# Seven block products instead of eight in six gate slabs of the mix part

## The reference

```python
u = rms_norm(h, mix_norm)
proj = u @ w_in                      # q, k, v, pool input, and 2 x 1024 gate columns
gates = sigmoid(proj[..., o:].reshape(B, S, 2, D_MODEL))
y_attn = dilated_mixture_attention(q, k, v) @ w_branch_attn      # 256 -> 1024
y_pool = multiscale_pool(pz, pool_w, pool_scale) @ w_branch_pool # 512 -> 1024
merged = gates[:, :, 0] * y_attn + gates[:, :, 1] * y_pool
h = h + merged @ w_out
```

## Time and profile before

| what | value |
|---|---|
| median of three executions | 1877.08 us |
| profiled execution, its own time | 1877.25 us |
| its span (first to last instruction) | 1875.0 us |
| TensorE busy | 1860.3 us, 99% |
| VectorE busy | 1294.7 us, 69% |
| ScalarE busy | 867.4 us, 46% |
| GpSimd busy | 46.5 us, 2% |
| granted TensorE clock, mean | 0.998 |

### The profile page before, as it was taken

One profiled execution on the slowest core, in us unless ns is written; L12 is line 12 of the kernel. 1 busy time (PEld: TensorE's weight loads), 2 busy tenths in 40 slices (PEclk: granted clock), 3 DMA queues, 4 the chain that ended last, 5 costly groups with the idle time before them and its releaser, 6 DMA issues.

```text
span 1875.0 us, 26603 instructions
## 1 busy us (share of the span) xinstructions
PE 1860.3 (99%) x10599; PEld 1626.1 (87%) x10599; DVE 1294.7 (69%) x1728; ACT 867.4 (46%) x1132; POOL 46.5 (2%) x60
## 2 busy tenths in 40 slices
PE   9999999999999999999999999999999999999997
PEld 7998998888888888988998888888888888888886
DVE  8875887887566578866888746364646786666666
ACT  6643664436353236633653242333336654454445
POOL 0000000000000000000000000000000000000000
PEclk9999999999999999999999999999999999999999
DMA  6734763311112235744753223221221222212213
GB/s 212 184 126 123 194 169 110 117 59 62 61 62 93 98 112 141 190 145 115 190 153 123 98 83 107 72 89 67 93 89 66 90 71 87 90 67 89 89 67 90
DMA packets 44382, 203.61 MB, mean 109 GB/s; under 512 B 5136, under 2 KB 6192, under 8 KB 32128
## 3 DMA queue, kind: packets, MB, share of 16 engines
q1 hardware_dynamic: 37088, 177.23, 27.6%
q0 software_dynamic: 6768, 24.50, 6.8%
q10 hardware_dynamic: 432, 0.56, 0.1%
HBM read 198.60 MB, written 3.67 MB: 108 GB/s over the span
## 4 chain that ended last, share of the span: by engine, by line
PE 96%; DVE 2%; ACT 1%; issue 0%; DMA 0%; DVEq 0%; ACTq 0%
PE acc L2205 22%; PE acc L2207 22%; PE acc L2206 22%; PE acc L2212 6%; PE acc L2211 6%; PE acc L2213 6%; PE att L2205 2%; PE att L2206 2%; PE att L2207 2%; PE att L2211 1%; PE att L2213 1%; PE att L2212 1%; PE acc L2442 1%; PE acc L2467 1%; DVE w_lo L1232 0%
## 5 line engine op out<-in xcount | busy, mean ns | idle before, releaser
L1232 DVE TENSOR_TENSOR w_lo<-raw,w_hi 128x2048 fp32r<-128x2048 f32 x126 | 286.9, 2277 | 76.6 <-ACT w_hi L580 75.8
L2205 PE MATMUL acc<-x_hi,w_hi 128*128 128x512 f32 x808 | 318.3, 394 | 0.9 <-DVE x_lo L1295 0.6
L2207 PE MATMUL acc<-x_hi,w_lo 128*128 128x512 f32 x808 | 314.9, 390 | 0.0
L2206 PE MATMUL acc<-x_lo,w_hi 128*128 128x512 f32 x808 | 314.7, 389 | 0.0
L580 ACT ACTIVATE w_hi<-raw 128x2048 fp32r<-128x2048 f32 x126 | 239.2, 1899 | 128.6 <-PE acc L2207 113.9
L2205 PEld LDWEIGHTS acc<-x_hi,w_hi 128*128 128x128 f32 x808 | 151.7, 188 | 36.0 <-issue 2.1
L2206 PEld LDWEIGHTS acc<-x_lo,w_hi 128*128 128x128 f32 x808 | 151.8, 188 | 32.4 <-issue 1.4
L2207 PEld LDWEIGHTS acc<-x_hi,w_lo 128*128 128x128 f32 x808 | 151.7, 188 | 31.9
L2205 PE MATMUL acc<-g_hi,w_hi 128*128 128x512 f32 x352 | 137.0, 389 | 0.0
L2206 PE MATMUL acc<-g_lo,w_hi 128*128 128x512 f32 x352 | 137.0, 389 | 0.0
L2207 PE MATMUL acc<-g_hi,w_lo 128*128 128x512 f32 x352 | 136.9, 389 | 0.0
(11 more groups left out here) (440 smaller groups left out, 4485.1 us busy)
## 6 DMA issues: line engine op xcount, KB each, us to landing
raw<-in_ret_head SPq DMA_DIRECT2D x24, 1024.0 KB, 4.8
raw<-in_ffn_down SPq DMA_DIRECT2D x32, 704.0 KB, 4.0
raw_c<-in_ffn_seven SPq DMA_DIRECT2D x37, 512.0 KB, 5.3
raw<-in_ffn_seven SPq DMA_DIRECT2D x33, 512.0 KB, 4.6
raw<-in_ffn_seven POOLq DMA_DIRECT2D x33, 512.0 KB, 7.5
raw<-in_ffn_seven SPq DMA_DIRECT2D x37, 256.0 KB, 4.5
raw<-in_mix_gate SPq DMA_DIRECT2D x8, 1024.0 KB, 4.8
raw<-in_ret_out SPq DMA_DIRECT2D x8, 1024.0 KB, 4.8
```

What stands on the lines that cost most here:

```text
L1232: tt(w_lo[:, slot, at:at + cols], raw[:, slot, 0:cols], w_hi[:, slot, at:at + cols].bitcast(F32), ALU.subtract).then_inc(w_ready, 1)
L2205: mm(dst, still[0], move[0], start=first, stop=False)
L2206: mm(dst, still[0], move[1], start=False, stop=False)
L2207: return mm(dst, still[1], move[0], start=False, stop=last)
```

## The change

Six of the eight gate slabs (those of the second, third and fourth pair) take seven products. Their weights are laid out in quarters (`mix_seven`), and fetched in three transfers a slab instead of one, with one accumulating transfer by GpSimd. The first pair stays as it was on TensorE.

- x's combinations for the mix: ScalarE writes gain x h, sorted, to `mix_top` and `mix_low` (8 activations); GpSimd makes four two-input operations of 1024 columns (`mix_forms`); ScalarE and VectorE split the results.
- The two sums of weights of each of the six slabs are made by GpSimd (`add_sums` in its program), not by VectorE as in the feed-forward parts.
- Of a branch slab only the 1536 columns that are used are split, not 2048. Three of its four results stay in PSUM (`att`) until they are multiplied.
- Each gate's early and late 256 tokens come from the four combinations of products (`blocks_of`), are scaled by the norm, and pass the sigmoid in two activations.
- SP holds back a branch slab, and the first slab of the output projection, until GpSimd's sums of the slot's last slab are made (`sum4_ready`).
- `dynamic_dma_scratch_size=4096` makes the room for descriptors of GpSimd's transfers smaller, and two unused tensors grow by 12 KB a partition.

```diff
@@ sync
+            for j in range(1, DC // 2):
+                if j > 1:
+                    sp.wait_ge(sum4_ready, v.k - 1)
+                fetch(dram["mix_branch"][j], 12 * BLK)
+                for k in range(2):
+                    w = dram["mix_seven"][2 * j + k - MIX_PLAIN]
+                    fetch_pair(w)
+                    fetch_one(w)
+                    if j == 1:
+                        sp.wait_ge(seg_done, FFN_SEGS[0] + GATES_FROM + 1)
+                    fetch_c(w)
+            sp.wait_ge(sum4_ready, v.k)
@@ gpsimd
+            def mix_forms():
...
+                pool.wait_ge(mix_x_ready, DC)
+                add(mix_form[:], b11, b12, ALU.subtract).then_inc(mix_formed, 1)
+                pool.wait_ge(mix_formed, 1)
+                add(b12, b12, b22, ALU.subtract).then_inc(mix_formed, 1)
+                add(b11, mix_form[:], b22, ALU.add).then_inc(mix_formed, 1)
+                pool.wait_ge(mix_formed, 3)
+                add(b21, b21, b11, ALU.subtract).then_inc(mix_formed, 1)
...
+            mix_forms()
+            for j in range(1, DC // 2):
+                for k in range(2):
+                    slab = FC + 2 * DC + BRANCH_FROM + 3 * j + 1 + k
+                    add_pair(dram["mix_seven"][2 * j + k - MIX_PLAIN], slab)
+                    add_sums(slab)
+                    v.next()
@@ scalar
+            for c in range(DC):
+                mix_x(c)
+            s.next(3)
+            sigmoid(0)
+            s.next(2)
+            u.next(2)
+            prep()
+            split_form(1, xt_hi[:, 0, :, :], mix_form[:])
...
+                for k in range(2):
+                    two, one = acc[:, u.k % BANKS, :], acc[:, (u.k + 1) % BANKS, :]
+                    split_sum4()
+                    if k:
+                        sigmoid_late()
+                        sigmoid_early()
+                    snap(1, t(0)[:, EARLY], two[:, EARLY])
+                    if k:
+                        split_val(m_hi[:, 2 * j, :], t(4))
+                    snap(2, t(0)[:, LATE], one[:, EARLY])
+                    if k == 0:
+                        split_pair()
+                    elif j < DC // 2 - 1:
+                        prep(12 * BLK)
+                    else:
+                        prep()
+                    snap(3, t(1)[:, EARLY], two[:, EARLY])
@@ vector
+                for k in range(2):
+                    if k:
+                        last_rows(0)
+                        late_product(pool_first)
+                    low_c()
+                    if k:
+                        early_product(attn)
+                    low_sum4()
+                    if k:
+                        low_mixed(2 * j)
...
+                    link(blocks_of(side))
+                    tt(t(3), t(3), rstd[:], ALU.mult).then_inc(val_ready, 1)
@@ tensor
+            for j in range(1, DC // 2):
+                w = slab()
+                branch_part(side_bank(), w, 2, (pool_hi, pool_lo), 4).then_inc(att_full, 1)
+                branch_part(side_bank(), w, 0, (o_hi, o_lo), 2).then_inc(att_full, 1)
+                branch_part(side_bank(), w, 8, (pool_hi, pool_lo), 4).then_inc(att_full, 2)
+                b.next()
+                side = att[:, (b.k - 1) % BANKS, EARLY]
+                project(w, 6, (o_hi, o_lo), 2)
+                for k in range(2):
+                    seven(6 if j == 1 and k == 0 else None, side)
```

More of the change, by code:

```diff
@@ L36 @@
 SNAPS = 4
+MIX_PLAIN = 2
+MIX_SEVEN = DC - MIX_PLAIN
 QUART = SLAB // PARTS
@@ L531, in _, with add_pair @@
                 pool.dma_start(dst if name == "signs" else dst[:], dram[name]).then_inc(const_landed, 16)
+            def add_pair(w, slab, ahead=None):
+                third = v.k % RING
+                pool.wait_ge(pair_landed[third], v.landed())
+                pool.dma_start(pair_place(slab % RING, ahead), w[:, QUART:3 * QUART],
+                               accum_op=ALU.add).then_inc(added_pair[third], 16)
             def add_pairs(name, full, first_slab):
@@ L932, in sigmoid, with mix_x @@
                 nc.scalar.activation(t(4 + o), t(4 + o), ACT.Sigmoid).then_inc(fn_ready, 1)
-            for i in range(DC // 4):
-                for j in range(2):
-                    if i or j:
-                        prep()
[L938 to L953, removed]
+            def mix_x(c):
+                dst = (mix_top if c < TB else mix_low)[:, c % TB, :]
+                nc.scalar.activation(sorted_row(dst), row_to_sort(h[:, c, :]), ACT.Copy,
+                                     scale=gains[:, 1, c:c + 1]).then_inc(mix_x_ready, 1)
@@ L1431, in seven, with blocks_of @@
                     low_one()
+                if ahead is not None:
+                    dve.wait_ge(pair_free, v.k)
+                blocks_of(att[:, snaps.k % BANKS, EARLY])
+            def blocks_of(side):
                 one = acc[:, (u.k + 1) % BANKS, :]
@@ L1434, in seven @@
                 dve.wait_ge(snap_ready, SNAPS * snaps.k + 1)
-                if ahead is not None:
-                    dve.wait_ge(pair_free, v.k)
-                tt(t(2)[:, EARLY], t(0)[:, EARLY], att[:, snaps.k % BANKS, EARLY], ALU.add).then_inc(dve_step, 1)
+                tt(t(2)[:, EARLY], t(0)[:, EARLY], side, ALU.add).then_inc(dve_step, 1)
                 dve.wait_ge(snap_ready, SNAPS * snaps.next())
@@ L1776, in _ @@
+            last_rows(0)
+            late_product(pool_second)
+            b.next(-2)
+            early_product(t(5))
+            low_mixed(DC - 1)
             nc.vector.memset(ssq[:], 0.0).then_inc(ssq_ready, 1)
@@ L2291, in product, with seven @@
                 ins.then_inc(done, 1)
-            def seven(first):
+            def seven(first, side=None):
                 pe.wait_ge(w_ready, n.at(RING + 1))
@@ L2313, in seven @@
                 pe.wait_ge(wc_ready, third + 1)
-                product(att[:, (v.k - 1) % BANKS, EARLY], a12, b21, True)
+                product(att[:, (v.k - 1) % BANKS, EARLY] if side is None else side, a12, b21, True)
                 pe.wait_ge(snap_ready, snap + 3)
@@ L2534, in _, with branch_part @@
             gather(u.at(BANKS), 2)
[L2535 to L2554, removed]
+            gate = slab()
+            project(gate, DC, x)
+            pe.wait_ge(att_free, b.at(BANKS))
+            for k in range(2):
+                project(branch[0], 6 * k, (o_hi, o_lo), 2)
+            project(gate, 0, x)
+            w = slab()
+            project(w, DC, x)
+            project(w, 0, x)
+            def branch_part(dst, w, first, still, chunks):
+                for c in range(chunks):
+                    ins = passes(dst, w(first + c), (still[0][:, c, :], still[1][:, c, :]), c == 0, c == chunks - 1)
+                return ins
+            for j in range(1, DC // 2):
+                w = slab()
+                branch_part(side_bank(), w, 2, (pool_hi, pool_lo), 4).then_inc(att_full, 1)
[4 more added lines that the diff above has]
+                project(w, 6, (o_hi, o_lo), 2)
+                for k in range(2):
+                    seven(6 if j == 1 and k == 0 else None, side)
             at = op.k
```

192 lines of the change are left out of this document (149 added, 43 removed).

## The result

The changed kernel took 1882.35 us in the median of 14 executions (1880.31 to 1885.0), the kernel before 1876.77 us in as many (1875.94 to 1877.72). The ratio of the two is 1.0031, 95% interval [1.0023, 1.0039]: slower by 5.6 us, 0.3%. The time lies inside the predicted range (1874.5 to 1885.5) and 2.4 us over the predicted 1880.0. But it lies outside the forecast's own, narrower range (1878 to 1881.5) and next to rival 1's 1882.7. The profiled execution took 1883.71 us, its span is 1881.9 us, its mean granted clock 0.995 (0.998 before).

A forecast was written before the change was run, and what follows sets the result against it. TensorE, busy 99% of the span, was taken as the bound; -8.1 + 6.7 + 2.2 + 0.5 + 1.4 = +2.7 us on 1877.25 gave 1880.0 us, range 1874.5 to 1885.5 (the forecast's own 1878 to 1881.5).

The forecast's parts named there:

- rival 1: VectorE and GpSimd exclude each other in full, costing 4.2 us: 1882.7 us, slower; chance 0.30.
- Saving: TensorE's pairs two to four cost 27.56 us each instead of 30.26: 8.1 us less over three pairs.
- New wait 1: Fifth product of each second slab, pairs two to four, waits for the third snapshot: 6.7 us in sum.
- Rival 2: Waits of ScalarE's order don't hold TensorE, only the first pair's and first seven-product slab's waits remain: 1871.9 us; chance 0.12.
- New wait 2: First pair's second gate slab: eight activations stand ahead of its copy on ScalarE, so TensorE waits 2.2 us.
- New wait 3: First seven-product slab: serial chain behind the gate's last matmul ends at 579.1, wanted at 578.6: 0.5 us stall.
- VectorE beside GpSimd: VectorE's two-input SBUF operations held while GpSimd reads, around the first pair: 0 to 4.2 us, a third taken, 1.4.
- The memset row: Profile row: beside GpSimd's memset, a VectorE add of two SBUF tensors took its usual 0.69 us.
- The clock: Granted clock is 1.00 in both windows read, so no clock term enters the sum.
- Rival 3: GpSimd's chain arrives last, with combinations over 3.3 us or the transfer over 10.5: 1883.6 to 1886 us; chance 0.13.
- scratch: Smaller descriptor scratch and the 12 KB shift cost nothing, as GpSimd's transfers are few.
- holds of SP: SP's holds on `sum4_ready` pass 6 us or more ahead of TensorE's need, so cost nothing.

The follow-up runs named there:

- e1_order: Changed kernel with ScalarE's split of the merged values m_hi moved behind the third snapshot in second gate slabs of pairs two to four; 1876.1 us.
- e3_noread: Changed kernel with GpSimd's sixteen two-input operations replaced by memsets of the same place, so GpSimd reads nothing; 1879.11 us.
- e5_spare: Changed kernel with spare matmuls, results unused, in TensorE's waits ahead of two first slabs and three fifth products; 1880.07 us.
- e4_scratch: Kernel before the change with only the smaller descriptor room (4096) and two unused tensors grown by 12 KB; 1875.73 us, ratio 0.9995.
- e6_both4: e1_order with four of the eight activations that write gain x h made by VectorE instead of ScalarE; 1871.58 us.
- e7_best: e6_both4 with the output projection's first slab taking chunks 0 to 6 of both outputs before chunk 7; 1870.61 us.

## Why the prediction was right, and where it wasn't

1. **Saving, 8.1 us.** Right. A seven-product slab took 9.74 and 9.71 us in pair three of e1_order (611.12 to 620.86 to 630.57; predicted 9.70). The branch slab there took 8.53 instead of 8.16, a small wait for a bank that shows only when TensorE is early.
2. **New wait 1, 6.7 us.** Right, in mechanism and size: 6.5 us, released by the snapshot behind the split and the copy, none in first slabs; moving the split took all three away. Rival 2 (the waits don't hold) is refuted.
3. **New wait 2, 2.2 us.** Right: 2.09 us in e3_noread, without GpSimd's share.
4. **New wait 3, 0.5 us.** Right: 0.45 us in e3_noread.
5. **VectorE beside GpSimd, 1.4 us.** The mechanism was named, the size was off. It measured 2.9 us where nothing covers it: 1.0 ahead of the gate slab and 1.9 in the chain to the first seven-product slab. The memset row, from which I shrank the upper bound of 4.2 us to a third, bears on writing only; the operations that read were the case. The Trainium skill (SBUF — State Buffer, "Who interferes with whom") had said so, and the trace agrees. My upper bound had left out the two multiplications beside GpSimd's third and fourth combination, which alone took 5.07 us instead of 1.47; the serial chain had room for a part of it. An exclusion has to be counted along the whole chain, not at the first meeting.
6. **The clock, no term.** This step failed, though the time stayed in its range. "The granted clock is 1.00 in both windows, so no term of the clock enters" took the clock from stretches in which TensorE never stood still, while my own sum put five standstills of up to 2.5 us there. Its price is 2.3 us in the medians (e5_spare) and 3.1 in the profiled executions; of the 5.0 us of slow matmuls the gate slab's 1.5 hid behind a wait that would have come anyway.
7. **Rival 3, scratch, holds of SP.** Right: no wait of TensorE was released by GpSimd or a transfer, and e4_scratch shows no change.

With 2.9 for 1.4 the sum without the clock is 4.2 us, and e5_spare measured 3.4 (1880.07 - 1876.69); with the clock's 2.3 it makes 6.5, and the changed kernel measured 5.6. The 0.9 us between them stay open. In the profiled executions the stretch from the first pair to the output projection grew by 7.9 us (115.46 to 123.39), while the rest of the span was 1.0 us shorter, which no term explains. So the forecast's 2.7 was short by two terms of the same sign, and its time stayed within 2.4 us since they were small. The range was wide enough to hold rival 1 too, so the time alone doesn't tell the two apart; the traces do. That the time falls on rival 1's 1882.7 is chance in good part: its mechanism, the exclusion, was there, but cost 2.9 us and not the full 4.2, and the rest of the way is the clock's.

## What to carry to other kernels

Where a change trades matmuls for waits, price the waits with the clock: here waits of 2.0 to 3.1 us on a TensorE that otherwise hardly rests cost up to 1.8 us again in the work behind them in six of ten cases, and waits of 1.0 to 1.4 us in none of seven. Order an in-order engine's queue by who is waited for: one 0.63 us instruction that sat ahead of a snapshot, for data that nobody needed for long, held up the copy and the snapshot behind it and cost 6.5 us over three slabs. When a wait goes, ask what it covered; here a wait of 1.0 us came up elsewhere.

## What the hardware showed that I had not expected

- The granted clock fell to 1.2 GHz behind waits of TensorE of 2.0 to 3.1 us, in the profiled executions behind three of four (changed kernel), one of two (e1_order) and two of four (e3_noread); behind waits of 1.0 to 1.4 us (one each in the changed kernel and e1_order, three in e6_both4, two in e7_best) and behind those filled with spare matmuls (e5_spare) never. None between 1.4 and 2.0 us was measured in this stretch. Two waits of the same 2.0 us in one execution differed in it (pairs two and three of e3_noread), and one of 3.0 us (e1_order) passed without, so it isn't the length alone that decides; what else does stays open. The Trainium skill (TensorE: Matmul & The Clock Gate, "Why this matters for your kernels") advises against longer idle gaps of TensorE between its matmuls. The traces agree only in part: the clock also fell behind gaps of 2.0 us, and did not behind every longer one.
- On the same kind of strided operand VectorE took 0.61 us for 512 columns where ScalarE took 1.12.
